# A two-layer network on one core: the delta rule's scan takes the inverse once per chunk, its last solve level runs on 64x64 corners, the mLSTM row chain moves into the solve, and columns are spread by transposes

## What is computed

```python
m = jnp.where(strict, einsum(k_beta, kc) * decay, 0.0); a = m + eye
rhs = concatenate([vc * bc, k_beta * jnp.exp(gc)], -1)
u, w = split(triangular_solve(a, rhs))            # a^-1 applied to both
def step(state, inp):                             # delta rule, one chunk
    v_new = u_i - w_i @ state
    o = (q_i * exp(g_i)) @ state + attn_i @ v_new
    state = state * exp(gl_i) + k_dec.T @ v_new
...
d_log = where(incl, b_i - b_j + i_j, -inf)        # mLSTM
m_t = maximum(b_i + m, max(d_log)); s = (q @ k.T) * exp(d_log - m_t)
h = num / maximum(abs(den), exp(-m_t))
```

## Time and profile before

| | |
|---|---|
| median of 3 runs | 2093.89 us (2093.67 to 2095.01) |
| profiled execution | 2092.58 us, its span 2090.8 us |
| mean granted PE clock | 0.978 |
| busy: PE, DVE, ACT, POOL | 1986.5, 727.5, 532.4, 117.7 us |

### The profile page before, as it was taken

How to read it: one execution, slowest core, us unless ns; L and a number is a source line. 1 busy time by engine, 2 the same in 40 slices (tenths; PEclk the granted TensorE clock), 3 DMA queues, 4 the chain that set the end, 5 groups by cost and what they waited for, 6 DMA issues and landing times.

```text
span 2090.8 us, 22450 instructions
## 1 busy us (share of the span) xinstructions
PE 1986.5 (95%) x9182; PEld 1241.8 (59%) x9182; DVE 727.5 (35%) x1045; ACT 532.4 (25%) x811; POOL 117.7 (6%) x127
## 2 busy tenths in 40 slices
PE   8999999999899998989899899999999999999998
PEld 6867843333232333323233378898778888887886
DVE  5648331101001010101001175763577544345324
ACT  5246320001010000001010155323444333234125
POOL 3431000000000000000000000141000000000000
PEclk9999999999999999999999999999999999999999
DMA  9421789999999999999999923111113222223231
GB/s 267 142 71 43 297 340 426 427 428 427 429 428 429 428 429 429 428 429 429 429 428 428 379 85 117 64 41 41 61 61 141 83 99 81 94 106 111 101 142 60
DMA packets 48741, 516.25 MB, mean 247 GB/s; under 512 B 5904, under 2 KB 6032, under 8 KB 13088
## 3 DMA queue, kind: packets, MB, share of 16 engines
q1 hardware_dynamic: 46496, 508.39, 59.7%
q0 software_dynamic: 2176, 6.88, 1.5%
HBM read 508.92 MB, written 6.29 MB: 246 GB/s over the span
## 4 chain that ended last, share of the span: by engine, by line
PE 71%; DMA 23%; DVE 3%; ACT 1%; issue 1%; SPq 0%; POOL 0%; DVEq 0%; ACTq 0%
DMA arena<-in_w_gu_dram 23%; PE bank L2423 13%; PE bank L2448 4%; PE bank L912 4%; PE bank L911 4%; PE bank L910 4%; PE bank L579 3%; PE bank L581 3%; PE bank L580 3%; PE bank L2386 2%; PE bank L942 2%; PE bank L944 2%; PE bank L943 2%; PE bank L2051 2%; PE bank L2057 2%; PE bank L2053 2%
## 5 line engine op out<-in xcount | busy, mean ns | idle before, releaser
L2423 PE MATMUL bank<-arena 128*64 128x512 f32 x2048 | 480.6, 624 | 70.7 <-DMA arena<-in_w_gu_dram 67.8
L2423 PEld LDWEIGHTS bank<-arena 128*64 128x64 f32 x2048 | 162.5, 143 | 364.0 <-issue 351.0
L2918 DVE TENSOR_TENSOR arena<-arena,bank 128x256 f32<-128x256 f32 x64 | 27.0, 421 | 642.8 <-ACT arena L3159 642.8
L2448 PE MATMUL bank<-arena 128*64 128x512 f32 x1024 | 232.5, 595 | 0.6 <-ACT arena L3163 0.6
L3159 ACT ACTIVATE arena<-bank 128x256 f32<-128x256 f32 x64 | 24.6, 384 | 539.3 <-PE bank L2423 539.3
L2448 PEld LDWEIGHTS bank<-arena 128*64 128x64 f32 x1024 | 73.4, 137 | 139.5 <-issue 139.5
L910 PE MATMUL bank<-input_rounded,weight_rest 128*128 128x512 f32 x352 | 137.1, 390 | 0.0
L912 PE MATMUL bank<-input_rounded,weight_rounded 128*128 128x512 f32 x352 | 136.9, 389 | 0.0
L911 PE MATMUL bank<-input_rest,weight_rounded 128*128 128x512 f32 x352 | 136.9, 389 | 0.0
L579 PE MATMUL bank<-input_rounded,weight_rest 128*128 128x512 f32 x312 | 126.0, 404 | 0.0
L580 PE MATMUL bank<-mix_rest,unit_rounded 128*128 128x512 f32 x312 | 122.3, 392 | 0.0
(11 more groups left out here) (522 smaller groups left out, 2924.4 us busy)
## 6 DMA issues: line engine op xcount, KB each, us to landing
arena<-in_w_gu_dram SPq DMA_DIRECT2D x126, 2048.0 KB, 26.9
arena<-in_w_d_dram SPq DMA_DIRECT2D x62, 2048.0 KB, 26.8
arena<-in_wpack_dram SPq DMA_DIRECT2D x83, 1024.0 KB, 4.9
arena<-in_w_d_dram SPq DMA_DIRECT2D x4, 1024.0 KB, 9.6
arena<-in_w_gu_dram SPq DMA_DIRECT2D x3, 1024.0 KB, 7.3
arena<-in_xT_dram SPq DMA_DIRECT2D x4, 512.0 KB, 7.0
arena<-in_x_dram SPq DMA_DIRECT2D x2, 1024.0 KB, 12.8
arena<-in_x_dram SPq DMA_DIRECT2D x1, 2048.0 KB, 8.2
```

The lines of the kernel that those rows point to most:

```text
L2423: last = mm(ab[64 * x:64 * x + 64, :], xsT[:, k, 64 * x:64 * x + 64], w[x][k], start=k == 0, stop=k == KD - 1)
L2448: last = mm(bank[4 + n][64 * x:64 * x + 64, :], hidT[c % 2][:, P * t + 64 * x:P * t + 64 * x + 64], w[:, x, t, 512 * n:512 * n + 512], sta ...
```

## The change

Five edits; the line numbers of the changed kernel are some tens higher.

1. Where columns are spread over a bank, before, the broadcast column was multiplied by the identity: once at the start (r1), at L648, at L920 and in each preparation (L687). These become transposes of the broadcast column. In the preparation `gc` (already summed) is turned instead of `gg` times the triangle `utri`. The maxima row of an mLSTM head becomes four transposes of a column of maxima, which is why a third set of four turns brings the maxima back to columns.
2. The last level (u 24 to 27) multiplies only the 64x64 corners that can differ from zero, copies and subtracts only these, and takes them straight from `maT`, so POOL makes no masked copies for it.
3. The scan no longer builds `kbg`, `wneg`. It computes keys times state (`ks`), subtracts it from `vbt` on DVE (`zed_made`, with -exp(g) beta), and applies the inverse once. In chunk 0 the state is zero, so its products are left out. Two `state` tiles alternate.
4. The mLSTM row chain runs inside the solve (PE at u=6 and u=14, DVE at u=6 to 16, ACT at u=17).
5. The mLSTM heads are pipelined: `expo` has two tiles; the next head's maxima, scores and exponents follow the current head's product with the values.

```diff
-            for u in range(5, 28):                      # POOL
+            for u in range(5, 24):
...
-                    mm(hv(bank[0], h), gg[:, n, h:h + 1].to_broadcast([P, P]), utri, start=True, stop=True)
+                    turn(hv(bank[0], h), gc[:, n, h:h + 1].to_broadcast([P, P]), ident)
...
+                        last = mm(hv(bank[n % 2], h)[64:128, 0:64], hv(maT[:, n, :], h)[0:64, 64:128],
+                                  hv(tin[:, n, :], h)[0:64, 0:64], start=True, stop=True)
...
+                        last = mm(hv(bank[2 + n % 2], h)[0:64, 64:128], hv(xw[n % 2], h)[64:128, 0:64],
+                                  hv(tit[:, n, :], h)[64:128, 64:128], start=True, stop=True)
...
+                if u == 6:
+                    pe.wait_ge(S("gg_made"), 4)
+                    for i in range(NT):
+                        turn(bank[4][0:4, P * i:P * i + P], lf[:, i, :], ident)
...
+                if u == 14:
+                    pe.wait_ge(S("mrow_made"), nth("mrow_made", 1))
+                    for i in range(NT):
+                        turn(bank[4][:, 4 * i:4 * i + 4], arow[0:4, P * i:P * i + P], ident[0:4, 0:4])
+                        turn(bank[4][:, 16 + 4 * i:20 + 4 * i], mxrow[0:4, P * i:P * i + P], ident[0:4, 0:4])
+                        last = turn(bank[4][:, 32 + 4 * i:36 + 4 * i], mrow[0:4, P * i:P * i + P], ident[0:4, 0:4])
...
             for n in range(4):
-                pe.wait_ge(S("tt_made"), 25 + n)
+                t = slice(P * n, P * n + P)
                 if n == 0:
-                    pe.wait_ge(S("aside_out"), N_ASIDE)
-                if n >= 2:
-                    pe.wait_ge(S("w_made"), nth("w_made", n - 1))
+                    pe.wait_ge(S("tt_made"), 27)
+                else:
+                    pe.wait_ge(S("st_made"), 4 * n - 3)
+                    for h in range(4):
+                        last = mm(hv(bank[3], h), qkv[:, 4 + h, t], hv(state[n % 2], h), start=True, stop=True)
+                    last.then_inc(S("ks_filled"), 1)
+                    gate_half(n, 0)
+                    pe.wait_ge(S("zed_made"), nth("zed_made", 4 * n))
                 for h in range(4):
-                    last = mm(hv(bank[6 + n % 2], h), hv(kbg[:, n, :], h), hv(tit[:, n, :], h), start=True, stop=True)
-                last.then_inc(S("w_filled"), 1)
...
-                    mm(hv(bank[7], h), hv(tit[:, n, :], h), hv(vbt[:, n, :], h), start=True, stop=False)
-                    last = mm(hv(bank[7], h), hv(wneg[:, n, :], h), hv(state, h), start=False, stop=True)
+                    last = mm(hv(bank[2], h), hv(tit[:, n, :], h), hv(vbt[:, n, :], h), start=True, stop=True)
                 last.then_inc(S("vn_filled"), 1)
-                gate_half(n, 0)
+                gate_half(n, 1 if n else 0)
                 pe.wait_ge(S("vn_made"), nth("vn_made", n + 1))
...
-                own(tt(out=h3(kbg[:, n, :]), in0=h3(bank[4][:, :]), in1=per_token(ebg, n), op=ALU.mult))
...
+                    dve.wait_ge(S("ks_filled"), nth("ks_filled", n))
+                    for h in range(4):
+                        stt(out=hv(vbt[:, n, :], h), in0=hv(bank[3], h), scalar=nebg[:, n, h:h + 1], in1=hv(vbt[:, n, :], h),
+                            op0=ALU.mult, op1=ALU.add).then_inc(S("zed_made"), 1)
+                    gate_scale(n - 1)
...
-                mm(bank[3][:, :], ident[0:4, h:h + 1].to_broadcast([4, P]), mxrow[0:4, :], start=True, stop=True)\
+                    last = turn(bank[3][:, P * i:P * i + P], mxcol[:, i, h:h + 1].to_broadcast([P, P]), ident)
...
+                if h < MH - 1:
+                    maxima_row(h + 1)
+                    head_scores(h + 1)
                 gate_half(6 + 2 * h, 0)
                 gate_half(6 + 2 * h, 1)
```

More of the change, by code:

```diff
@@ L807, in second_pe @@
                 last.then_inc(S("ms_filled"), 1)
-                if h == 0:
-                    pe.wait_ge(S("mx_made"), 1)
+            maxima_row(0)
+            gate_half(4, 0)
+            pe.wait_ge(S("sg_scaled"), 4)
+            head_scores(0)
+            gate_half(4, 1)
+            pe.wait_ge(S("mv_one"), 1)
+            pe.wait_ge(S("oa_made"), nth("oa_made", 4))
+            for h in range(MH):
                 gate_half(5 + 2 * h, 0)
@@ L1235, in second_dve, with exponents @@
-            own.wait()
             offs = (0, 512, 896, 1152)
             where = ((4, 0), (5, 0), (6, 0), (5, 384))
+            def exponents(h):
+                dve.wait_ge(S("mb_filled"), nth("mb_filled", h + 1))
+                for a in range(NT):
+                    ts(expo[h % 2][:, offs[a]:offs[a] + L - P * a], bank[3][:, P * a:L], acol[:, a, h:h + 1], 0.0,
+                       ALU.subtract, ALU.max).then_inc(S("mx_made"), 1)
+            gate_scale(3)
+            dve.wait_ge(S("mcol_copied"), nth("mcol_copied", 1))
@@ L1246, in second_dve @@
-                if h:
-                    gate_scale(4 + 2 * h)
-                dve.wait_ge(S("me_made"), nth("me_made", h + 1))
-                for a in range(NT):
-                    own(tt(out=expo[:, offs[a]:offs[a] + P], in0=expo[:, offs[a]:offs[a] + P], in1=utri, op=ALU.mult))
+                    own(tt(out=e[:, offs[a]:offs[a] + P], in0=e[:, offs[a]:offs[a] + P], in1=utri, op=ALU.mult))
                 own.wait()
@@ L1254, in second_dve @@
                     b, o = where[a]
-                    e = expo[:, offs[a]:offs[a] + L - P * a]
-                    own(tt(out=e, in0=e, in1=bank[b][:, o:o + L - P * a], op=ALU.mult))
+                    part = e[:, offs[a]:offs[a] + L - P * a]
+                    own(tt(out=part, in0=part, in1=bank[b][:, o:o + L - P * a], op=ALU.mult))
                 own.wait()
                 dve.engine_nop().then_inc(S("mp_made"), 1)
+                gate_scale(4 + 2 * h)
                 gate_scale(5 + 2 * h)
+                if h < MH - 1:
+                    exponents(h + 1)
                 dve.wait_ge(S("mo_filled"), nth("mo_filled", h + 1))
@@ L1598, in gate_out @@
                 fn(sg[f], sg[f], ACT.Sigmoid).then_inc(S("sg_made"), 1)
-            for n in range(4):
-                act.wait_ge(S("w_filled"), nth("w_filled", n + 1))
-                fn(wneg[:, n, :], bank[6 + n % 2][:, :], ACT.Copy, scale=-1.0).then_inc(S("w_made"), 1)
             for n in range(4):
@@ L2090, in _ @@
             for i in range(NT):
[L2091 removed]
+                last = turn(bank[0][:, P * i:P * i + P], r1[:, i:i + 1].to_broadcast([P, P]), ident)
             last.then_inc(S("sq1_summed"), 1)
```

199 lines of the change are left out of this document (103 added, 96 removed).

## The result

The changed kernel takes 2070.32 us (median of four runs, 2069.57 to 2071.79); the kernel before took 2093.78 beside it (2092.49 to 2095.01). The ratio is 0.9888, its 95% interval 0.9876 to 0.9900: 23.5 us less by the medians, 20.8 by the two profiled executions (2092.58 and 2071.79). In another series the changed kernel took 2071.58 beside 2094.85, ratio 0.9888 again. Single executions of the same code differ by 1 to 2 us; for smaller things I use the trace, and there a "stretch": from the first matmul of the r13 row (L648 before) to the first product of the second layer's branches. It is 356.9 us before, and 336.6 and 336.5 in two profiles of the changed kernel. (The expectations of experiments 1, 3, 7 and 8 count to a matmul 0.4 later, 337.0.)

What follows compares the result with a forecast made beforehand. PE was taken to bound the kernel, busy 1986.5 of 2090.8 us (95%). The terms summed to 21.8 us off the profiled 2092.58, leaving 2070.8; with 1.3 for the median, 2072.1 us, range 2069 to 2077.5.

Steps and rivals of the forecast that it cites:

- columns, preparation (with `kbg` gone): Preparation: a transpose saves 0.112 us per block; 2.68 in chunks 1 to 3 and 0.60 in chunk 0.
- columns, three rows: Rows at the start (r1), L648 and L920: twelve blocks at 0.112 us, 1.34 saved, the three taken to be alike.
- corners: Last solve level: 64 instructions at 0.06 us save 3.3, less eight shape changes at 0.1: net 2.5.
- row chain: mLSTM row chain in the solve: a wait of 0.80 goes, four new small turns cost 0.26, net 0.54.
- between solve and scan: Window between solve and scan: all 6.37 us go, 3.57 of work (L756) and 2.8 of waits.
- the scan: Scan: 17 groups of 0.893 us instead of 19, 1.79 saved.
- heads 1 to 3 (three maxima and waits): mLSTM heads: transposed maxima save 0.60 us each, and 2.0 of waits before the product with the values go; 3.8.
- head 0's maxima and clock: Head 0: maxima save 0.60 us, and no fall to 1.2 GHz behind its scores saves 1.6; 2.2.
- Case (a): Whole kernel: the covers hold and it takes 2072.1 us, own range 2070 to 2075; chance 0.70.
- there is some lead, and I take it that it covers 0.3 per chunk: Preparation, later chunks: DVE's lead covers PE shortening by 0.89 us against DVE's 0.60; 0.9 is the worst.
- The covers that I called thin: Scan: other PE work hides new waits of 1.4 us; the state's cover is thinnest, 0.4.
- rival (c): Clock falls elsewhere, 1.6 us per stretch at 1.2 GHz; one or two give 2073.7 to 2075.3; chance 0.12.

Runs made afterwards that it cites:

- experiments 1: Changed kernel with the last solve level on full 128x128 blocks again, POOL's masked copies included: 2074.74 us, stretch 339.1.
- 3: Changed kernel with the preparation's columns multiplied by identity and triangle again instead of transposed: 2073.05 us, stretch 338.4.
- 7: Changed kernel whose first scan product waits for the solve's last subtraction and last aside, as before: 2072.41 us, stretch 337.8.
- experiment 8: Changed kernel with the next head's maxima and scores behind the gate unit: 2080.58 us, stretch 345.4.
- 4: Changed kernel with the preparation's scaling of the values moved from DVE to ACT: 2070.96 us beside the changed kernel's 2071.58.
- Experiment 6: Changed kernel with the scan of before (`kbg`, `wneg`, one state tile, 19 groups): 2081.77 us, ratio 0.9938 to the kernel before.
- experiment 12: Changed kernel with the first row (r1) alone spread by multiplying with the identity again: 2072.68 us, r13 row starting at 1223.7.
- experiment 2: Changed kernel with each of the 64 corner products run twice, no border between shapes added: 2075.17 us, stretch 340.0.
- experiment 9: Changed kernel with the row chain's twelve small turns moved from the solve to straight ahead of head 0: 2071.12 us, stretch 336.8.
- 10: `rows_late`: experiment 9 with the turns to rows and DVE's row chain also moved behind the scan: 2079.88 us, stretch 341.7.
- 11: As 10, with head 0's maxima spread by a product as in the kernel before, not four transposes: 2074.85 us, stretch 340.1.

## Why the prediction was right, and where it wasn't

The sum was made of eight terms; by the traces they come to this, in us.

| term | foreseen | measured |
|---|---|---|
| columns, preparation (with `kbg` gone) | 3.28 | 3.4, less a new wait of 0.92: 2.5 |
| columns, three rows | 1.34 | 0.4, 0.4 and (r1) not to be told |
| corners | 2.5 | 2.5 |
| row chain | 0.54 | 0.3 |
| between solve and scan | 6.37 | 6.37 |
| the scan | 1.79 | 1.77 (38.94 to 37.17) |
| heads 1 to 3 (three maxima and waits) | 3.8 | 4.3 (78.57 to 74.23) |
| head 0's maxima and clock | 2.2 | 2.1 |
| sum | 21.8 | 20.6 without r1; profiles 20.8 |

**Case (a) came, at its forecast time**: 2070.3 and 2071.6 against 2072.1. The profiled execution was foreseen at 2070.8 and took 2071.8. By the profiled executions the sum was 1.0 too high. The medians lie 1.8 and 0.5 below the forecast all the same, because the profiled execution was 1.3 below the median before and is 1.5 above it here; that is the scatter of single executions, and so luck.

**Columns by transposes.** 0.89 a chunk of PE's work went, as the half price of the earlier trace rows has it. The step that failed is "there is some lead, and I take it that it covers 0.3 per chunk". I read the lead from an idle time of 0.76 in the whole preparation, but where PE shows no gap, DVE need have no lead. In the kernel before, POOL's copies were ready 0.04 us ahead of PE's second step. With each of the three later chunks 0.89 shorter on PE and only 0.60 on DVE, 3 x 0.29 = 0.87 was missing there, and the 0.92 came out through POOL at the second solve step: exactly the "0.9 at worst" that I had put aside. Experiments 3, 4 and 6 show the cause from three sides: more work for PE hides it, 0.6 less on DVE per chunk removes it, and 0.6 more doubles it.

**r1.** I took its 0.45 to be worth its length. In the changed kernel the experts' stage behind it has 72.0 us of idle PE, 69.0 of them for weights by the groups of instructions, so I take it that PE's early end has nothing to shorten there. Two profiles of the changed kernel speak for it: the experts' first product at 285.1 and 285.9, the r13 row at 1222.8 and 1222.7 (286.1 and 1222.9 before). It isn't shown, since experiment 12 drowned in the scatter.

```profile
L2467 PE MATMUL bank<-arena 128*64 128x512 f32 x2048 | 480.3, 624 | 72.0 <-DMA arena<-in_w_gu_dram 69.0
```

**Corners.** 2.5 is right, and its parts are not. The price of a product is 0.056 to 0.058 (experiment 2), so the products alone save 3.5; a border costs more than my 0.1: a run of eight with its two takes 0.09 ahead (0.53 for the four turns of L762 before it, in place of 0.44), 0.15 inside and 0.11 behind, 0.17 each, 1.4 for eight. What brings the sum back is that the two kinds run beside each other where they meet: the run of two groups takes 0.89 where its products and 0.15 inside would be 1.05, the run of four 1.77 for 1.94, 0.3 in all. 7.14 - 3.58 - 1.4 + 0.3 = 2.5. The two errors cancel, and that is luck. The rule of the Trainium skill that I weighed first (that a change of mode drains the engine) agrees in kind. The second (a floor per matmul) can't show at 64 columns, which take half of 128; it agrees in kind with the turns of four columns, which at 0.062 take no less than a product of 64. The Trainium skill says in "TensorEngine Tiling (Array Packing)", Key Properties, that different tiles can run in parallel; the pairs of starts 0.01 apart agree, since the one kind goes from rows 0-63 to columns 64-127 and the other the opposite way.

**The row chain.** Foreseen: a wait of 0.80 against four small turns. All twelve take 0.83 us in the solve, and 0.2 at their borders, which I left out: 0.80 + 0.52 - 0.83 - 0.2 = 0.3. In the new order the twelve turns could as well stand at head 0: there they cost 0.2 (experiment 9). The rows' chain can't, but that is by the banks of the outputs and the clock, not by the wait of 0.80.

**Between solve and scan, and the scan.** Right to 0.02. The covers that I called thin held: the state's update starts 1450.66 and PE comes to the product that needs it at 1452.24, the cover 0.4 as foreseen. Experiment 6 gives 7.7 for both terms (8.16 foreseen), the difference being shorter waits at the old place, and 7 says which of the waits was bought by order alone (1.2).

**Heads.** 0.5 more than foreseen. A head takes 16.14 in each case, in place of 17.47, 17.61 and 17.58. The product with the values, the maxima and the scores now stand in one run, with fewer changes of shape, and the product no longer follows a wait; that this is the 0.5 is argued, not shown. With the next scores behind the gate unit DVE doesn't keep up (experiment 8: 6.7 us of waits).

**The clock.** The fall of the earlier trace rows is gone, and the term held to 0.1. But my reading of it ("waited 0.80 and run eight small turns, L801 and L805") is only a part. Twelve small turns, four transposes and the scores with a wait of 0.42 among them ran at full clock (experiment 9); with 1.5 us of idle time one gate unit earlier a fall came, with the product for the maxima too (10 and 11); and a fall came right behind 2.62 us of idle time that a full gate unit preceded (8), though not behind 2.35 or 1.77 in the other heads. Idle time of PE stood ahead of every fall, but not every idle time brought one; why it falls in one head and not in the next is open, and each of these versions ran once. The rival (c) did not come. My argument against it misread the second window of the earlier trace rows: of its 28 matmuls only 16 are transposes, 1.7 us in a row between matmuls of full units, so it showed less than I took from it. In the changed kernel 12 small turns, 64 quarter-array products and all the transposes ran with 1.00 granted.

## What to carry to other kernels

Take the price of a group from start to start at the place, and check a reordering term by term; such sums hold to a few tenths. What they miss is the engine without gaps that has no lead either: before an edit shortens PE's part of a stage, follow the other engine's list over that stage, and compare the two lengths. Its own waits belong to the list: DVE is busy for only 38.84 of the preparation's 48.20 us, and by busy time alone it would seem to have 9 to spare, but in each chunk it also waits for ACT (6.7 us in all). Best is to read at the stage's end how long before PE's need the other engine was ready, 0.04 us here. The deficit collects and comes out later, under another engine's name. And put a half of other work ahead of each wait: it was worth 1.2 us here, and idle PE may cost the clock on top of the wait.

## What the hardware showed unexpectedly

- Float32 products of 64x64 that use opposite corners of the array start 0.01 us apart where both kinds are in the queue, though each alone takes 0.056 to 0.058.
- The granted clock fell to 0.50 for over 4.4 us (the rest of a unit at 0.43 a matmul in place of 0.23) in `rows_late`, where the version without the wait of 1.5 us behind the scan kept 1.00 (one execution of each): 3.2 us were lost to slower work.
- A turn of four columns takes 0.062 us (L750 to L752, start to start, in the solve), more than an instruction of a product of 64 columns (0.056).
